# Order of one attention stage in a two-block kernel: transposes and value product behind each step's query or output unit, the first mask ahead of two weight splits

## The reference

```python
q = (h @ w_q).reshape(bsz, L, N_HEADS, HEAD_DIM)
...
s = jnp.einsum("bhqd,bhkd->bhqk", qb, k).astype(jnp.float32) * scale
s = s + cq[..., :, None] - c[..., None, :]
s = jnp.where(mask, s, NEG_INF_2)
p = jax.nn.softmax(s, axis=-1)
return jnp.einsum("bhqk,bhkd->bhqd", p.astype(v.dtype), v)
...
return o @ w_o
```

## Time and profile before

| | us |
|---|---|
| median of 3 executions | 1857.22 |
| lowest and highest | 1855.72 and 1857.57 |
| the profiled execution | 1856.42 |
| its span in the trace | 1853.7 |

### The profile page before, as it was taken

The page is one execution under the profiler, slowest core; times in us unless marked ns, Lnnn a source line. Parts: engine busy times, 40 slices in busy tenths (PEclk is TensorE's granted clock), DMA queues, the critical chain, the costliest instruction groups (busy, mean ns, idle before and its releaser), DMA issues.

```text
span 1853.7 us, 33296 instructions
## 1 busy us (share of the span) xinstructions
PE 1803.3 (97%) x14354; PEld 1759.8 (95%) x14354; DVE 1137.9 (61%) x1806; ACT 976.5 (53%) x1536; POOL 123.6 (7%) x128
## 2 busy tenths in 40 slices
PE   8889999999999999999999999999999999899998
PEld 8778999998889999999999999999999999899998
DVE  6656788655367886565555766554555555665554
ACT  6555666556436665554444446443554444665443
POOL 1001000110012001100011020001100002020002
PEclk9999999999999999999999999999999999999999
DMA  6233455544415555455554544555444554236553
GB/s 215 95 114 108 165 188 182 187 165 161 142 42 187 183 186 189 170 168 174 171 180 147 174 148 162 179 172 175 152 168 159 182 186 167 91 119 199 183 184 101
DMA packets 85042, 297.77 MB, mean 161 GB/s; under 512 B 10496, under 2 KB 13440, under 8 KB 84896
## 3 DMA queue, kind: packets, MB, share of 16 engines
q1 hardware_dynamic: 82400, 294.16, 47.5%
q10 hardware_dynamic: 2496, 1.49, 0.3%
HBM read 294.57 MB, written 1.05 MB: 159 GB/s over the span
## 4 chain that ended last, share of the span: by engine, by line
PE 87%; DVE 7%; ACT 3%; issue 1%; POOL 1%; DMA 1%; ACTq 0%; SPq 0%; DVEq 0%; POOLq 0%
PE ps L1327 28%; PE ps L1329 27%; PE ps L1328 27%; PE ps L1374 1%; POOL acc L798 1%; DVE w_lo L829 1%; ACT w_hi L379 1%; DMA raw<-stream 1%; DVE y L865 1%; ACT a_hi L421 1%; ACT x L417 0%; PE ps L1528 0%; DVE y L877 0%; PE ps L1709 0%; DVE tmp L907 0%
## 5 line engine op out<-in xcount | busy, mean ns | idle before, releaser
L829 DVE TENSOR_TENSOR w_lo<-raw,w_hi 128x1024 fp32r<-128x1024 f32 x557 | 692.7, 1253 | 403.2 <-ACT w_hi L379 277.0
L1327 PE MATMUL ps<-a_hi,w_hi 128*128 128x256 f32 (+1 forms) x2336 | 667.5, 286 | 8.6 <-DVE a_lo L1089 3.6
L379 ACT ACTIVATE w_hi<-raw 128x1024 fp32r<-128x1024 f32 x557 | 580.1, 1051 | 177.8 <-DMA raw<-stream 154.5
L1329 PE MATMUL ps<-a_hi,w_lo 128*128 128x256 f32 (+1 forms) x2336 | 663.0, 284 | 0.0
L1328 PE MATMUL ps<-a_lo,w_hi 128*128 128x256 f32 (+1 forms) x2336 | 662.5, 284 | 0.0
L1327 PEld LDWEIGHTS ps<-a_hi,w_hi 128*128 128x128 f32 x2336 | 441.8, 189 | 15.4 <-issue 8.0
L1329 PEld LDWEIGHTS ps<-a_hi,w_lo 128*128 128x128 f32 x2336 | 442.1, 189 | 0.0
L1328 PEld LDWEIGHTS ps<-a_lo,w_hi 128*128 128x128 f32 x2336 | 440.2, 188 | 0.2
L1327 PE MATMUL ps<-h_hi,w_hi 128*128 128x256 f32 (+1 forms) x1376 | 389.9, 283 | 6.4 <-DVE h_lo L1240 3.6
L1329 PE MATMUL ps<-h_hi,w_lo 128*128 128x256 f32 (+1 forms) x1376 | 389.2, 283 | 0.0
L1328 PE MATMUL ps<-h_lo,w_hi 128*128 128x256 f32 (+1 forms) x1376 | 388.7, 282 | 0.0
(11 more groups left out here) (233 smaller groups left out, 1526.9 us busy)
## 6 DMA issues: line engine op xcount, KB each, us to landing
raw<-stream SPq DMA_DIRECT2D x557, 512.0 KB, 3.3
x<-xT SPq DMA_DIRECT2D x1, 1024.0 KB, 7.0
out<-x SPq DMA_DIRECT2D x8, 128.0 KB, 1.7
work<-pT ACTq DMA_DIRECT2D x2, 256.0 KB, 2.7
par<-params ACTq DMA_DIRECT2D x1, 283.5 KB, 4.6
tmp<-causal ACTq DMA_DIRECT2D x1, 208.0 KB, 2.5
con<-consts ACTq DMA_DIRECT2D x1, 194.5 KB, 6.3
tmp<-pos ACTq DMA_DIRECT2D x1, 128.0 KB, 14.9
```

Of the source, the lines that this page charges most:

```text
L379: nc.scalar.activation(w_hi[:, u % SLOTS, :], raw[:, u % SLOTS, :], ACT.Copy).then_inc(w_hi_ready, 1)
L829: nc.vector.tensor_tensor(w_lo[:, u % SLOTS, :], raw[:, u % SLOTS, :], w_hi[:, u % SLOTS, :].bitcast(F32), ALU.subtract).then_inc(w_lo_rea ...
L1327: nc.tensor.matmul(dst, wh, xh, start=first, stop=False, skip_group_check=True)
L1329: return nc.tensor.matmul(dst, wl, xh, start=False, stop=last, skip_group_check=True)
```

## The change

Within each step, PE now takes scores of head i + 2 and the query or output unit first, and the transposes of head i and the value product of head i - 1 after them. ACT's order follows: exponentials, query copy and weight split first, then the copies of the transposes and the high part. On DVE one weight split instead of three stands ahead of the loop; the other two come behind the mask of the first head. In all later steps DVE's weight split stands ahead of the low part of head i - 1 instead of behind it, and step 2 has two splits. No instruction is added or removed.

```diff
@@ ACT
             for i in range(-2, 9):
                 a = 16 + i
+                if i + 2 < 8:
+                    exponentials(a + 2, 144, 272, sm_a)
+                if i + 5 < 8:
+                    query(i + 5)
+                if 3 <= i < 6:
+                    hi_next(BASE["att_o"] + i - 3)
                 if 0 <= i < 8:
                     act.wait_ge(turned, a + 1)
...
-                if i + 2 < 8:
-                    exponentials(a + 2, 144, 272, sm_a)
-                if i + 5 < 8:
-                    query(i + 5)
-                if 3 <= i < 6:
-                    hi_next(BASE["att_o"] + i - 3)
@@ DVE
-            for n in range(3):
-                lo_next(BASE["att_q"] + n)
+            lo_next(BASE["att_q"])
             dve.wait_ge(cq_copied, 1)
             for i in range(-2, 9):
                 if i + 2 < 8:
                     masked(i + 2, 16, 144, 272, sm_a, mask_c, False)
                 if 0 <= i + 1 < 8:
                     normalized(16 + i + 1, 144, 272, sm_a)
+                for n in {-2: (1, 2), -1: (3,), 0: (4,), 1: (5,), 2: (6, 7)}.get(i, ()):
+                    lo_next(BASE["att_q"] + n)
+                if 3 <= i < 6:
+                    lo_next(BASE["att_o"] + i - 3)
                 if 1 <= i:
                     mixed_low(16 + i - 1, H_SPLIT["att"] + i, i - 1, 2 + (16 + i - 1) % 2)
-                if i + 5 < 8:
-                    lo_next(BASE["att_q"] + i + 5)
-                if 3 <= i < 6:
-                    lo_next(BASE["att_o"] + i - 3)
@@ PE
             for i in range(-2, 9):
-                if 0 <= i < 8:
-                    att_turn(i)
                 if i + 2 < 8:
                     att_scores(i + 2)
-                if 1 <= i:
-                    att_mix(i - 1)
                 if i + 5 < 8:
                     att_query(i + 5)
                 elif i >= 3:
                     att_out(i - 3)
+                if 0 <= i < 8:
+                    att_turn(i)
+                if 1 <= i:
+                    att_mix(i - 1)
```

## The result

| | before | after |
|---|---|---|
| median, us | 1857.01 | 1860.34 |
| lowest to highest, us | 1855.72 to 1858.04 | 1857.63 to 1863.17 |
| executions | 14 | 14 |
| the profiled execution and its span, us | 1856.42, 1853.7 | 1861.27, 1859.0 |

The ratio after to before is 1.0020, 95% interval 1.0013 to 1.0028. The forecast was +2.2 us (1859.4), its range 1855.4 to 1863.0. Before, the executions spread over 2.3 us, after over 5.5 us.

What follows compares the result with a forecast made beforehand. PE, 97% busy, bounds the kernel through its stops and clock; the start's lead is lost to a 3.4 us stop and 5.95 us rings, net +2.2: 1856.42 becomes 1858.6, plus 0.8 for the median 1859.4, range 1855.4 to 1863.0.

Steps and rivals of the forecast that it cites:

- The start gains: Stage start: one split before head 0's mask puts it at 1584.1, not 1586.56; PE's 4.2 us stop and clock fall go.
- Value product of head 0 waits 0.4: PE, ready for head 0's value product at 1597.6, waits 0.4 us for ACT's copies, done at 1598.0.
- A new stop of 3.4 before the first output part, ending 1608.7: PE waits 3.4 us for the fourth output unit's weight split, from 1605.2 to 1608.7; before, 0.33 us.
- The ring of 5.95: Later steps: transposes, mask, exponentials, weight high part, split, low part, next transposes; 5.95 us per step against 4.61 before.
- Sum +2.2 from the order: Last output part ends at 1638.1 instead of 1635.9, +2.2 us, with no clock fall in the new stops.
- No DMA joins the path: Loads: a load lands in 4.2 us, every unit is split over 5 us after its release, so none delays the stage.
- The clock: Rival: clock falls to 1.2 GHz in the new stop; once +3.2, worst +4.2, chance 0.22; again and again, chance 0.10.
- no fall: The forecast case, clock staying full in the new stops: +1 to +3 us, chance 0.45.
- again and again: Rival: clock also falls in the 2.2 to 2.9 us stops; rings 0.6 each, tail 1.7; +5 to +8 us, chance 0.10.
- a stop must exceed some 3.6 us: Ground for a full clock: PE stops of 3.64 and 4.21 were followed by falls, 0.8 waits not; new stop 3.4.
- The page's rule: Throttled by default, activity releases; so trading one long stop for four of 2.2 to 3.4 us is more open to falls.
- The page's price: Throttled time multiplied by 1 - K/N: 1.7 us for a 3.4 us fall, making the sum with one fall +3.9.

Runs made afterwards that it cites:

- first-mask run: Kernel before with only the second and third weight split moved behind the first head's mask: 1853.92 us, -3.1 us.
- Undoing the ring in two ways: Changed kernel with ACT's old order and DVE's low part ahead of the split: 1854.22 us; or with query copy and weight's high part ahead of exponentials: 1855.08 us.
- clock held at full: Changed kernel with idle PE products (12, 7, 7 and 10) in its four long stops: 1858.66 us, +1.45 us against the kernel before.
- the run with the ring undone: Changed kernel with ACT's order as before and DVE's low part ahead of the split again: 1854.22 us, -2.9 us against the kernel before.
- two others: Kernel before with two splits moved behind the first mask (stop 1.85): 1853.92 us; with ACT's query copy and weight's high part ahead of exponentials (1.89): 1852.28 us.
- fitting partners: PE's loop of the changed kernel with ACT's and DVE's loops of the new pipeline: 1849.05 us, -8.2 us against the kernel before.
- all three loops together: New pipeline: PE, ACT and DVE loops rewritten with the same instructions so no step waits for itself: 1846.52 us, -10.7 us against the kernel before.

## Why the prediction was right, and where it was not

- *The start gains.* Right: first mask at 1584.10 (1584.1 said), no stop where the 4.2 us one had been, and full clock through 1600. Alone it is worth 3.1 us (first-mask run).
- *Value product of head 0 waits 0.4.* It waited 0.47.
- *A new stop of 3.4 before the first output part, ending 1608.7.* 3.34, ending 1608.64, released by a weight split.
- *The ring of 5.95.* It measured 6.00 to 6.04 from turn to turn. The short side was DVE's reaction to the transposes: 0.85, where I had taken ACT's 0.77, inside my 0.6 to 0.9. Undoing the ring in two ways took 6.2 and 5.5 us off the changed kernel, and brought the transposes from 6.0 to 4.3 to 4.9 us apart, so it is shown to be the cause of the order's loss.
- *Sum +2.2 from the order.* With the clock held at full the median is +1.45 (+0.2 to +3.3), the profiled stage +2.6. The term stands, within an interval that is wider than itself.
- *No DMA joins the path.* No stop of PE in the stage was released by one.
- *The clock.* This is where the likeliest case was wrong. I gave "no fall" 0.45 and "again and again" 0.10; the profiled execution, +4.9, is the latter, just under its +5 to +8. One part of that rival failed: it had falls in the rings cost 0.6 each, and the one that came there cost nothing; the one in the tail cost 2.7, where it had 1.7. The term that +2.2 put at nothing measured 1.9 us in the median. That the median still came out only 1.1 over the forecast is partly luck, since by the same medians the order measured 0.75 below its +2.2; and the range, 7.6 us wide, held everything from no change to this. My ground for it, that a stop must exceed some 3.6 us, fell: the clock stayed up behind the 3.34 us stop and was down behind the next, of 2.10 us. The same 3.34 us stop had a fall in the run with the ring undone; stops of 1.85 and 1.89 us in two others had none and one. The length of a stop does not decide by itself. What else does is open.
- *The page's rule.* The Trainium skill (TensorE: Matmul & The Clock Gate, Part 1, section What's actually happening) says that the throttled state is the default and that activity releases it. What I drew from it, that four stops open a kernel to falls more than one does, agreed with the trace (two falls in the stage, 10.2 us, against one of 3.4) better than my reading of the rows did; I should have given that rival more than 0.32 in all. The page's price (section Terms), half of the throttled time, gives an estimate of 5.1 us for the stage's 10.2 us at half clock. Measured were 2.7: the 3.4 us from 1617.2 lay in time that PE would have waited, and so did the first 0.8 of the other 6.8.

## What to carry to other kernels

In a software pipeline over several engines, write down for each recurring wait the ring it closes, over all engines' orders, and sum it: the longest ring is the period, and an order on one engine is good or bad only with the others': PE's changed one measured -8.2 us with fitting partners, +3.3 and +8.3 with others. Work that nobody in this step needs, such as the next weight's high part, belongs ahead of work that waits for another engine. On ACT that alone gave 4.7 and 5.5 us, in all three loops together 10.7. On DVE alone it did not help: the split ahead of the low part, while ACT still made the weight's high part last, went with a loss of 6.2 us. I put that down to the split's own input being late; no run separates it. And count what a stop of the matrix engine can do to the clock apart from its length, even at 2 us: a fall costs nothing where PE would wait anyway (from 1617.2), and nearly half its length where PE has work (1.5 us of 3.4 in the kernel before, 2.7 of 6.8 in the tail).

## What the runs showed of the hardware that I had not expected

- An idle product of 128 x 128 in full 32 bits appears as two PE instructions, 0.115 us apart (48 for 24 in 5.52 us); the weight products, with rounded operands and twice the columns, go at 0.12 us each. Per column, full 32 bits cost nearly four times as much here (0.23 us for 128 against 0.12 for 256).
- Falls of the clock to 1.2 GHz in the stage began in a stop or up to 1.3 us behind its end, with stops of 1.89 to 4.65 us, each 3.4 or 6.8 us long, and not with every stop of a length: stops of 2.63, 2.77 and 3.34 us had none.
- At full clock DVE in the changed kernel starts 0.81 to 0.85 us after the start of the transposes that it waits for, ACT 0.77.
